# Moving three waits in a fused two-block transformer kernel: one forget product per level, diagonal copies ahead, first heads on the first query fill

## The chip, the cores and the metric

The kernel runs on one core of one Trainium2 chip. The metric is the device time of one execution in microseconds; 972.3 us is the median of three runs before the change (971.54, 972.3, 977.76).

## What is computed

Two transformer blocks over 256 tokens of width 1024, in float32. The first (convolution and retention, then a feed-forward and a gated projection) is not touched. The second normalises x and multiplies it by one wide input matrix; the columns of the product feed three branches, which are merged, projected and followed by a convolutional feed-forward. The branch of the change is HGRN2, a gated linear attention that runs forwards and backwards over the tokens, 8 heads of 128:

```python
h = rmsnorm_2(x, norm_mix[l])
(hq, hi, hff, hfb, hg, nq, nk, nv, cq, g_hg, g_na, g_ca) = split_cols(h @ w_in[l])
y_hg = hgrn2_branch(hq, hi, hff, hfb, hg, lower_bounds[l], hg_gnorm[l], w_hg_o[l])
y_na = neighbourhood_attention(nq, nk, nv, na_rpb[l], w_na_o[l])
y_ca = memory_cross_attention(cq, mem_n, w_mem_kv[l], w_ca_o[l])
...
# in hgrn2_branch, for either direction
f = lb_d + (1.0 - lb_d) * jax.nn.sigmoid(zf)
log_f = jnp.log(jnp.maximum(f, F_FLOOR))
k = (1.0 - lb_d) * jax.nn.sigmoid(-zf)
...
# in gla_chunk_scan: token t sees token s through the product of the forgets between them
scores = jnp.einsum('bhtk,bhsk,bhtsk->bhts', qc, kc, decay)
```

The cross attention is ordinary: 4 heads of 128, queries cq, keys and values from a memory of 256 tokens. The neighbourhood attention has 8 heads of 64.

## The kernel before

**Weights.** They stream from memory in units of 8 blocks of 128 x 128 (raw). ScalarE casts a unit to its high part w_hi (L627), DVE (L1022) or POOL (L590) subtracts to get the low part w_lo, and TensorE multiplies high and low parts in three passes. Four units are held (w_hi, w_lo), so the cast of a unit waits until TensorE has used the one four before it. A "fill" is the product of h with the weights of one piece of the columns (16 blocks, 48 matmuls) into one of three PSUM banks (ring), and an engine reads the bank out. On ScalarE, `wait_fill` casts the units up to a target (`split_target`), waits for the fill, and casts those that its end has set free (`behind_target`).

**The order of the second block.** The fills come in the order hq, hff, hfb (queries and forgets), then the sixteen "side fills" hi 0 to 3, hg 0 to 3, nq, nk, nv, cq (two each), then the merge fills mhg, mca, mna (eight each). Every engine runs through the same list of side fills and does its part of the HGRN2 scores between them, by `DIAGONAL_AFTER = 1`, `LEVEL_AFTER = {1: 0, 3: 1, 5: 2, 7: 3, 9: 4, 11: 5, 12: 6}` and `CROSS_AFTER = 13`. So after fill hi 1 come the diagonal and level 0, after hi 3 level 1, after hg 1 level 2, and so on.

**The levels.** The scores of two tokens are built by halving: at level i (half width b = 1, 2, ..., 64) the token pairs that lie in the two halves of a span of 2b are filled in. The steps of a level:
- ScalarE, `level_keys`: waits until the forgets and keys of the level are there (`level_ready`), then makes the mixed keys in two copies (L683, into gate_tmp and k_mix). It sits in `wait_fill`, ahead of the wait for the fill.
- TensorE, `level`: 64 small matmuls in four groups (L1831) into four banks (sc); group g waits for its key copy and, at level 0, for ScalarE's copy of the diagonal of that group (`st_diag`), later for DVE's masks of the level before.
- DVE, `masks`: copies the banks under a mask into st_hg (L1344), eight in all. `grow`: four products of 1024 elements carry queries and keys to the next level (L1360 to L1363), a wait for the last of them, and then the forget product of the forward direction (L1364) and of the backward direction (L1365), every 2b-th element by its partner b further on; the second one signals `level_ready`.

The diagonal (`diagonal` on TensorE, L1811, 16 products) stands right behind fill hi 1 and ahead of level 0; on ScalarE its four copies (L864) stand behind the weight cast and the value copy of hi 1 (L700).

**After the levels.** `cross` and `hg_values` give the outputs o_hg, which DVE gates and normalises (L1379, L1385, L1389) and splits (L1036) for the fill mhg 0. Fills cq 0 and cq 1 follow on TensorE; ScalarE copies each into its half of q_ca (L700). The attention heads go in slots between the merge fills, four cross heads first (`att_slot`): scores of a head (L1898), DVE's maximum (L1414, L1416), ScalarE's exponential (L915), DVE's normalisation (L1421, L1423), TensorE's transposes (L1908) and, a slot later, its products with the values (L1933, L1923). Head i reads head i's part of q_ca; fill cq 0 holds heads 0 and 1. Slot 0 stands between fill cq 1 and fill mhg 0.

SyncE loads a table for the neighbourhood attention once the last forget product has been signalled; POOL masks it between low parts.

Of the kernel before, what the change touches and what calls it, by code (L numbers as in the profile page):

```python
# [198 lines left out]
def program(nc, x_tok, mem_tok, pt, wstream, wproj, vecs, gains, consts, rope_tab, decay_tab, rpb, out, toep):  # L199
    ctx = ExitStack()  # L200
    with ctx:
# [43 lines left out]
        def at(kib, name, *shape, dt=F32):  # L245
            assert 1024 * kib + 4 * np.prod(shape) <= 1024 * ARENA_KIB, name
            return place(name, list(shape), dt, offset=arena + int(1024 * kib))
# [27 lines left out]

        f_f = at(0, "f_f", HG, S)
        f_b = at(8, "f_b", HG, S)
        k_fb = at(16, "k_fb", 2, HG, S)
# [177 lines left out]
        def wait_read(eng, name, j):  # L456

            n = fi(name, j)
            eng.wait_ge(freed[FILLS[n][3]], freed_count(n, FILLS[n][3]))
# [154 lines left out]
        def _(act):  # L614
# [61 lines left out]
            def level_keys(i):  # L676


                b = LEVELS[i]
                act.wait_ge(level_ready, i + 1)  # L680
                for half in range(2):
                    dst = k_mix[half].rearrange("p a s -> p (a s)").rearrange("p (n two b) -> p n two b", two=2, b=b)
                    nc.scalar.copy(dst, partners(k_f[:, 4 * half:4 * half + 4], b)).then_inc(mix_keys, 1)  # L683

            def wait_fill(name, j, behind=True):

                n = fi(name, j)
                feed(split_target(n))
                side = n - fi("hi", 0)
                if side in LEVEL_AFTER:  # L690
                    level_keys(LEVEL_AFTER[side])
                act.wait_ge(pe_step, fill_step(n))
                if behind:
                    feed(behind_target(n))
# [194 lines left out]

            for e, (name, j) in enumerate(SIDE_FILLS):  # L890
                if name in ("hi", "nv"):
                    dst = (v_hg if name == "hi" else v_na)[:, :, 256 * j:256 * j + 256]
                    copy_fill(name, j, dst)
                elif name == "hg":
                    copy_fill(name, j, gate_hg[:, 2 * j:2 * j + 2], ACT.Silu)
                else:
                    copy_fill(name, j, {"nq": q_na, "nk": k_na, "cq": q_ca}[name][:, 2 * j:2 * j + 2])
                if e == DIAGONAL_AFTER:
                    diagonal()
                if e == CROSS_AFTER:  # L900
                    cross()
                    hg_outputs()
                if e >= CROSS_AFTER:
                    hg_hi_part(e - CROSS_AFTER)
# [88 lines left out]
        def _(dve):  # L993
# [353 lines left out]
            def grow(i):  # L1347
# [7 lines left out]
                nb = HG * S // (2 * b)  # L1355
                fa, fb_ = halves(f_f[:])
                ba, bb_ = halves(f_b[:])
                bc = lambda t: t[:, :, 0:1].to_broadcast([P, nb, b])
# [4 lines left out]
                after(link(V.tensor_tensor(kb, kb, bc(ba), ALU.mult)))  # L1363
                V.tensor_tensor(fa[:, :, 0:1], fa[:, :, 0:1], fb_[:, :, 0:1], ALU.mult)  # L1364
                V.tensor_tensor(ba[:, :, 0:1], ba[:, :, 0:1], bb_[:, :, 0:1], ALU.mult).then_inc(level_ready, 1)  # L1365
                dve.wait_ge(level_ready, i + 2)
# [172 lines left out]
        def _(pe):  # L1539
# [339 lines left out]
            def att_scores(a):  # L1879
# [12 lines left out]
                if a < 2:  # L1892
                    pe.wait_ge(hg_root, 4)
                    wait_read(pe, "cq", 1)
                else:
                    pe.wait_ge(exp_ready, a - 1)
                for t in range(2):
                    last = mm(sc[a % 2][:, t * S:t * S + S], q_ca[:, i, t * P:t * P + P], mem_k[:, i, :],  # L1898
                              start=True, stop=True)
# [195 lines left out]
```

## Time and profile before

| | |
|---|---|
| median of three runs | 972.3 us |
| profiled execution | 973.71 us, of which 971.9 us span |
| TensorE busy | 936.8 us, 96% |
| DVE, ScalarE, POOL busy | 688.4, 518.2, 371.1 us |
| mean granted TensorE clock | 0.995 |

How to read it: the levels stand between 478 and 585 us, the merge fills with the heads between 607 and 703. The page's shares are averages over the whole program, and TensorE is the busiest engine in nearly every slice; what an edit is worth is read from the pieces of the chain of waits in its own stretch, and from the brackets in an engine's timeline, which say how long it was idle before an instruction and what released it. A piece called "issue" waited for nothing that the profile names. Matmuls are pipelined, so a matmul's row may start before the one ahead of it has ended.

### The profile page before, as it was taken

To read this page: it belongs to the slowest core of one execution; us is meant where nothing else is said; L and a number is where in the kernel's file an instruction comes from. 1 tells how busy PE (TensorE), PEld (TensorE's weight loads), DVE (VectorE), ACT (ScalarE), POOL (GpSimd) and SP (SyncE) were. 2 spreads that over 40 slices of the span, in tenths; PEclk is the share of its full clock that TensorE was granted. 3 is DMA by queue.
4 is the path that set the end of the run, shared out by engine and by line. 5 is a ranking of instruction groups with operands and counts; after the bars stand their busy time and mean duration, and the time that the engine had idled before them with its cause. 6 is when DMAs were issued, how large, how long until landed. Compare 5 with 4: busy or idle time off the path is not lost.

```text
span 971.9 us, 15074 instructions
## 1 busy us (share of the span) xinstructions
PE 936.8 (96%) x6118; PEld 848.7 (87%) x6118; DVE 688.4 (71%) x886; ACT 518.2 (53%) x790; POOL 371.1 (38%) x136
## 2 busy tenths in 40 slices
PE   7999999999999999999999999999899999999997
PEld 6998986888888878999999998999799878888885
DVE  4998586688884257567598977875545569999722
ACT  6853465545444356555444445554544556666632
POOL 0000000556664400002555533555686236566541
PEclk9999999999999999999999999999999999999999
DMA  9652344555556544545523325443355455555551
GB/s 354 216 204 87 141 136 161 202 176 195 193 174 216 176 171 174 174 171 177 174 87 131 130 93 157 152 142 130 102 194 204 137 176 186 182 207 175 185 205 44
DMA packets 30437, 162.57 MB, mean 167 GB/s; under 512 B 9089, under 2 KB 9489, under 8 KB 11936
## 3 DMA queue, kind: packets, MB, share of 16 engines
q1 hardware_dynamic: 30304, 161.53, 48.4%
q8 instruction: 49, 0.80, 0.3%
q14 instruction: 20, 0.16, 0.1%
q0 software_dynamic: 64, 0.08, 0.0%
HBM read 160.48 MB, written 1.12 MB: 166 GB/s over the span
## 4 chain that ended last, share of the span: by engine, by line
PE 86%; DVE 8%; ACT 4%; issue 2%; DMA 1%; SPq 0%; DVEq 0%; ACTq 0%
PE ring L1579 28%; PE acc L1657 18%; PE acc L1591 9%; PE ring L1591 8%; PE ring L1610 5%; PE acc L1592 4%; PE ring L1592 4%; PE acc L1831 3%; PE acc L1692 1%; ACT w_hi L627 1%; DVE w_lo L1022 1%; DVE y L1074 1%; DMA gain_mix_pre<-gains 1%; PE ring L1692 1%; DVE ret_inv L1185 1%
## 5 line engine op out<-in xcount | busy, mean ns | idle before, releaser
L590 POOL TENSOR_TENSOR w_lo<-raw,w_hi 128x1024 fp32r<-128x1024 f32 x124 | 359.2, 2902 | 580.3 <-ACT w_hi L627 580.2
L627 ACT CAST w_hi<-raw 128x1024 fp32r<-128x1024 f32 x284 | 296.7, 1050 | 322.3 <-PE ring L1579 120.4
L1022 DVE TENSOR_TENSOR w_lo<-raw,w_hi 128x1024 fp32r<-128x1024 f32 x160 | 202.6, 1275 | 107.2 <-ACT w_hi L627 97.0
L1579 PE MATMUL ring<-h,w_hi 128*128 128x256 f32 x1408 | 257.4, 285 | 3.7 <-DVE w_lo L1022 1.8
L1579 PEld LDWEIGHTS ring<-h,w_hi 128*128 128x128 f32 x1408 | 219.7, 192 | 6.7 <-issue 3.1
L1579 PE MATMUL ring<-h,w_lo 128*128 128x256 f32 x704 | 199.1, 283 | 0.0
L1579 PEld LDWEIGHTS ring<-h,w_lo 128*128 128x128 f32 x704 | 135.0, 192 | 0.0
L1591 PE MATMUL acc<-h,w_hi 128*128 128x512 f32 x352 | 125.9, 400 | 2.9 <-DVE h L1080 2.9
L1591 PE MATMUL ring<-h,w_hi 128*128 128x512 f32 x352 | 124.2, 396 | 0.0
L1592 PE MATMUL acc<-h,w_lo 128*128 128x256 f32 x352 | 99.0, 281 | 0.0
L1592 PE MATMUL ring<-h,w_lo 128*128 128x256 f32 x352 | 98.2, 279 | 0.0
L1657 PE MATMUL acc<-w_hi,ff 128*128 128x512 f32 x352 | 94.3, 390 | 0.0
L1591 PEld LDWEIGHTS acc<-h,w_hi 128*128 128x128 f32 x352 | 66.9, 190 | 19.4 <-DVE h L1080 2.0
L1591 PEld LDWEIGHTS ring<-h,w_hi 128*128 128x128 f32 x352 | 66.1, 188 | 15.9
L1657 PEld LDWEIGHTS acc<-w_hi,ff 128*128 128x128 f32 x352 | 65.8, 188 | 13.8 <-DVE w_lo L1022 0.2
L1241 DVE TENSOR_TENSOR ff<-prod_tmp,ff 128x256 fp32r<-128x256 f32 x44 | 67.2, 1529 | 0.9 <-ACT ff L985 0.9
L1592 PEld LDWEIGHTS acc<-h,w_lo 128*128 128x128 f32 x352 | 67.0, 190 | 0.0
L1592 PEld LDWEIGHTS ring<-h,w_lo 128*128 128x128 f32 x352 | 66.3, 188 | 0.0
L1657 PE MATMUL acc<-w_lo,ff 128*128 128x512 f32 x176 | 54.2, 389 | 0.0
L1610 PE MATMUL ring<-w_hi,h 128*128 128x256 f32 x256 | 46.9, 285 | 0.8 <-ACT v_ret L700 0.8
L1248 DVE TENSOR_REDUCE ring<-acc 128x512 f32<-128x1024 f32 x22 | 27.1, 1233 | 22.2 <-PE acc L1592 22.2
L1610 PEld LDWEIGHTS ring<-w_hi,h 128*128 128x128 f32 x256 | 40.0, 192 | 1.1 <-ACT v_ret L700 1.0
(251 smaller groups left out, 1395.0 us busy)
## 6 DMA issues: line engine op xcount, KB each, us to landing
raw<-wstream SPq DMA_DIRECT2D x142, 1024.0 KB, 4.8
toep_t<-toep SPq DMA_DIRECT2D x16, 96.0 KB, 3.2
x<-x_tok SPq DMA_DIRECT2D x2, 512.0 KB, 5.2
mem<-mem_tok SPq DMA_DIRECT2D x1, 1024.0 KB, 12.4
w_ple<-wproj SPq DMA_DIRECT2D x1, 1024.0 KB, 7.4
out_t<-y SPq DMA_DIRECT2D x4, 256.0 KB, 2.4
decay<-decay_tab SPq DMA_DIRECT2D x1, 768.0 KB, 7.2
gain_mix_pre<-gains SPq DMA_DIRECT2D x1, 512.0 KB, 7.2
```

Of the source, the lines that this page charges most:

```text
L590: nc.gpsimd.tensor_tensor(w_lo[:, u % UNITS], unit_of_raw(u), as_f32(w_hi[:, u % UNITS]), ALU.subtract).then_inc(lo_ready["pool"], 1)
L627: nc.scalar.copy(w_hi[:, u % UNITS], unit_of_raw(u)).then_inc(hi_ready, 1)
L1022: V.tensor_tensor(w_lo[:, u % UNITS], unit_of_raw(u), as_f32(w_hi[:, u % UNITS]), ALU.subtract).then_inc(lo_ready["dve"], 1)
L1241: V.tensor_tensor(ff[:, 1, j], prod_tmp[:, j % 2], as_f32(ff[:, 0, j]), ALU.subtract).then_inc(ff_ready, 1)
L1248: V.tensor_reduce(bank(name, j), b.rearrange("p i a s -> p i s a"), AX.X, ALU.add).then_inc(summed, 1)
L1579: last = mm(dst, w[a], src[:, b, kt], start=n == 0 and i == 0, stop=n == kts - 1 and i == 2)
L1591: mm(both, w[0], h_both[:, kt].rearrange("p a s -> p (a s)"), start=kt == 0, stop=False)
L1592: last = mm(b[:, i, 0], w[1], h[:, 0, kt], start=False, stop=kt == KT - 1)
L1610: last = mm(b[:, tt], src[:, xa, kt, tt * P:tt * P + P], ws[kt][wa], start=kt == 0 and i == 0, stop=kt == KT - 1 and i == 2)
L1657: last = mm(acc[:, tt, 512 * g:512 * g + 512], src(b, i, tt), w[:, u % UNITS, 4 * g:4 * g + 4].rearrange("p a b -> p (a b)"), start=i == 0 ...
L1692: last = mm(out, diag[:, w], conv_in[:, t, w:w + S], start=w == first, stop=w == end - 1)
L1831: last = mm(sc[g][:, c:c + P], tile(k_mix[g // 2], 2 * (g % 2) + a, tt), q, start=True, stop=True)
```

## The change

Three edits:

1. f_f and f_b become the two halves of one tensor f_fb at the same addresses. The two forget products of a level become one of twice the elements, and that one signals `level_ready`.
2. ScalarE waits for fill hi 1 and makes the four diagonal copies first; the cast that the end of the fill sets free and the value copy follow. `level_keys` counts its calls, so that the second `wait_fill` for the same fill does not repeat the keys.
3. TensorE's scores of heads 0 and 1 wait for ScalarE's read of fill cq 0 instead of cq 1; the wait for cq 1 moves to head 2.

```diff
-        f_f = at(0, "f_f", HG, S)
-        f_b = at(8, "f_b", HG, S)
+        f_fb = at(0, "f_fb", 2, HG, S)
+        f_f, f_b = f_fb[:, 0], f_fb[:, 1]
...
             def level_keys(i):
 
+                level_keys.done += 1
...
+            level_keys.done = 0
+
             def wait_fill(name, j, behind=True):
...
-                if side in LEVEL_AFTER:
+                if side in LEVEL_AFTER and LEVEL_AFTER[side] == level_keys.done:
                     level_keys(LEVEL_AFTER[side])
...
             for e, (name, j) in enumerate(SIDE_FILLS):
+                if e == DIAGONAL_AFTER:
+                    wait_fill(name, j, behind=False)
+                    diagonal()
                 if name in ("hi", "nv"):
...
-                if e == DIAGONAL_AFTER:
-                    diagonal()
                 if e == CROSS_AFTER:
...
-                fa, fb_ = halves(f_f[:])
-                ba, bb_ = halves(f_b[:])
+                fa, fb_ = halves(f_f)
+                ba, bb_ = halves(f_b)
...
-                V.tensor_tensor(fa[:, :, 0:1], fa[:, :, 0:1], fb_[:, :, 0:1], ALU.mult)
-                V.tensor_tensor(ba[:, :, 0:1], ba[:, :, 0:1], bb_[:, :, 0:1], ALU.mult).then_inc(level_ready, 1)
+                both = f_fb[:].rearrange("p d a s -> p (d a s)").rearrange("p (n two b) -> p n two b", two=2, b=b)
+                first, second = both[:, :, 0, 0:1], both[:, :, 1, 0:1]
+                V.tensor_tensor(first, first, second, ALU.mult).then_inc(level_ready, 1)
...
                 if a < 2:
                     pe.wait_ge(hg_root, 4)
-                    wait_read(pe, "cq", 1)
+                    wait_read(pe, "cq", 0)
                 else:
                     pe.wait_ge(exp_ready, a - 1)
+                if a == 2:
+                    wait_read(pe, "cq", 1)
```

ScalarE around the diagonal, behind the fill hi 1, before the change:

```order
L627 CAST w_hi<-raw 128x1024 [waits pe_step,slot_ready0]
L683 COPY gate_tmp<-k_fb 128x1024 [waits level_ready]
L683 COPY k_mix<-k_fb 128x1024
L627 CAST w_hi<-raw 128x1024 [waits pe_step]
L700 COPY v_hg<-ring 128x2x256
L864 COPY st_hg<-acc 128x2x2x128 [waits sc_done] x4
L627 CAST w_hi<-raw 128x1024 [waits pe_step,slot_ready1]
```

and with the change (lines have moved by some):

```order
L627 CAST w_hi<-raw 128x1024 [waits pe_step,slot_ready0]
L685 COPY gate_tmp<-k_fb 128x1024 [waits level_ready]
L685 COPY k_mix<-k_fb 128x1024
L868 COPY st_hg<-acc 128x2x2x128 [waits sc_done,pe_step]
L868 COPY st_hg<-acc 128x2x2x128 [waits sc_done] x3
L627 CAST w_hi<-raw 128x1024 [waits pe_step]
L704 COPY v_hg<-ring 128x2x256
```

The four copies into st_hg have passed one cast and one value copy; the first cast and the key copies stay where they were.

DVE at the end of level 1, before (q_bf and k_fb are the queries and keys of both directions, f_f and f_b the forgets):

```order
L1360 TENSOR_TENSOR q_bf<-q_bf,f_f 128x512x2
L1361 TENSOR_TENSOR k_fb<-k_fb,f_f 128x512x2
L1362 TENSOR_TENSOR q_bf<-q_bf,f_b 128x512x2
L1363 TENSOR_TENSOR k_fb<-k_fb,f_b 128x512x2
L1364 TENSOR_TENSOR f_f<-f_f 128x512 [waits dve_chain]
L1365 TENSOR_TENSOR f_b<-f_b 128x512
L1022 TENSOR_TENSOR w_lo<-raw,w_hi 128x1024 [waits hi_ready,level_ready]
```

and with the change:

```order
L1365 TENSOR_TENSOR q_bf<-q_bf,f_fb 128x512x2
L1366 TENSOR_TENSOR k_fb<-k_fb,f_fb 128x512x2
L1367 TENSOR_TENSOR q_bf<-q_bf,f_fb 128x512x2
L1368 TENSOR_TENSOR k_fb<-k_fb,f_fb 128x512x2
L1371 TENSOR_TENSOR f_fb<-f_fb 128x1024 [waits dve_chain]
L1027 TENSOR_TENSOR w_lo<-raw,w_hi 128x1024 [waits hi_ready,level_ready]
```

Two products of 512 elements have become one of 1024, and nothing else has moved; the other levels differ in the same way.

## Rows read from the trace of the kernel before

**Rows 1.** The page, part 1: busy us (share of the span) and instructions.
```profile
PE 936.8 (96%) x6118; PEld 848.7 (87%) x6118; DVE 688.4 (71%) x886; ACT 518.2 (53%) x790; POOL 371.1 (38%) x136
```
**Rows 2.** Chain of waits, 455 to 640 us: start us, us, what.
```profile
479.16 5.53 PE acc L1831 x32
484.69 11.50 PE ring L1610 x96
496.19 0.86 issue
...
529.42 0.57 issue
...
570.02 1.14 issue
```
**Rows 3.** TensorE's timeline: start us, us, instruction, [idle before <-releaser].
```profile
475.75 2.40 PE L1811 MATMUL acc<-y,sq 128*128 128x128 f32 x20
...
514.10 2.02 PE L1831 MATMUL acc<-q_bf,gate_tmp 128*128 128x128 f32 x16 [1.46 <-issue]
```
**Rows 4.** ScalarE's timeline, 470 to 590 us.
```profile
477.01 1.04 ACT L627 CAST w_hi<-raw 128x1024 fp32r<-128x1024 f32 x1
...
478.44 2.02 ACT L864 COPY st_hg<-acc 128x512 f32<-128x512 f32 x4
...
495.81 1.15 ACT L683 COPY gate_tmp<-k_fb 128x1024 f32<-128x1024 f32 x1
...
509.86 1.05 ACT L627 CAST w_hi<-raw 128x1024 fp32r<-128x1024 f32 x1
...
526.63 1.05 ACT L627 CAST w_hi<-raw 128x1024 fp32r<-128x1024 f32 x1 [1.33 <-PE ring L1579]
```
**Rows 5.** DVE's timeline at the ends of levels 1, 4 and 5.
```profile
505.25 1.22 DVE L1363 TENSOR_TENSOR k_fb<-k_fb,f_b 128x1024 f32<-128x1024 f32 x1
506.50 3.20 DVE L1364 TENSOR_TENSOR f_f<-f_f 128x512 f32<-128x512 f32 x1
...
554.51 2.37 DVE L1364 TENSOR_TENSOR f_f<-f_f 128x64 f32<-128x64 f32 x1
...
569.64 0.23 DVE L1364 TENSOR_TENSOR f_f<-f_f 128x32 f32<-128x32 f32 x1
```
**Rows 6.** POOL's timeline in levels 0 and 1.
```profile
478.13 2.36 POOL L590 TENSOR_TENSOR w_lo<-raw,w_hi 128x1024 fp32r<-128x1024 f32 x1 [3.06 <-ACT w_hi L627]
...
505.23 6.73 POOL L590 TENSOR_TENSOR w_lo<-raw,w_hi 128x1024 fp32r<-128x1024 f32 x2 [3.73 <-ACT w_hi L627]
```
**Rows 7.** Chain of waits at the first heads.
```profile
608.34 0.49 ACT q_ca L700
...
616.69 0.44 PE acc L1908 x4
...
623.75 0.44 PE acc L1908 x4
```
**Rows 8.** DVE's timeline at the first heads.
```profile
611.26 1.45 DVE L1036 TENSOR_TENSOR o_hg_s<-o_hg,o_hg_s 128x512 fp32r<-128x512 f32 x2
...
614.81 0.62 DVE L1423 TENSOR_SCALAR probs<-probs,soft 128x256 f32<-128x256 f32 x2
...
620.76 1.76 DVE L1423 TENSOR_SCALAR probs<-probs,soft 128x256 f32<-128x256 f32 x2
```
**Rows 9.** TensorE's timeline among the heads.
```profile
608.97 1.10 PE L1898 MATMUL acc<-mem_k,q_ca 128*128 128x256 f32 x4 [1.77 <-ACT q_ca L700]
...
675.33 1.08 PE L1923 MATMUL acc<-probs_t,v_na 128*64 128x256 f32 x8
...
689.47 1.12 PE L1908 MATMUL acc<-con,probs 128*128 128x128 f32 x4 [2.59 <-DVE probs L1423]
690.52 1.98 PE L1923 MATMUL acc<-probs_t,v_na 128*64 128x256 f32 x8
```
**Rows 10.** Busy us of PE, PEld, DVE, ACT, POOL; granted clock; DMA share, GB/s.
```profile
690.00:693.00 3.00, 3.00 (x15) 1.54 (x14) 2.67 (x4) 0.26 (x1) 2.35 (x1) 0.60 0.00 0
```

## The prediction

> **What bounds the kernel now.** I read the page's first part, then the chain of waits in the two stretches that the change touches, and last the engines' own timelines there. TensorE is busy 96% of the span [rows 1]. So an edit is worth only what it takes out of TensorE's gaps; a cheaper DVE or ACT operation in a covered stretch is worth nothing. The reader should see in the chain [rows 2] how few gaps there are: TensorE's level products (L1831) alternate with fills (L1610, L1579). Ahead of level 0 it waits 1.01 us, from 478.15, where the diagonal products end (475.75 + 2.40 in [rows 3]), to 479.16. Ahead of level 1 the "issue" piece is 0.86 us, of level 3 0.57, of level 6 1.14 [rows 2]. Ahead of level 2 the chain runs over DVE, so the gap is the bracket of [rows 3], 1.46 us. Levels 4 and 5 have none to speak of. Together that is 5.0 us. The second touched place is the first cross head, ahead of which TensorE is idle for 1.77 us [rows 9]. The whole reach of the change is thus 6.8 us, 0.7% of the time.
>
> **Diagonal copies ahead of weight and value.** Nothing is added on ScalarE or taken from it; the four L864 copies (2.02 us together) move ahead of a weight cast (1.04 us) and a value copy. Before, the key copies end as the cast starts, at 477.0, and the first diagonal copy starts at 478.44 [rows 4]; level 0 starts when it has landed, at 479.16. Afterwards the first diagonal copy starts near 477.1 and ends near 477.7. TensorE is busy with the diagonal products until 478.15, and ScalarE's pitch of 0.5 us is shorter than a group of level 0 (5.53 / 4 = 1.4 us), so the later groups do not wait either: **1.0 us** gained. The cast starts near 479.1 in place of 477.01. Queued behind it is POOL's low part of the same unit (2.36 us from 478.13 [rows 6]), which then ends near 482.6. Its reader is the fill hi 3, half way through the 11.50 us piece that begins at 484.69 [rows 2], near 490.4: 7.8 us of cover. The value copy frees a bank that is wanted only three fills after its own. Both moves cost nothing; with that cover gone, the price would be the 2.1 us of the move.
>
> **One forget product per level.** DVE loses seven instructions of 886. What counts is when the last product ends, since ScalarE's key copies wait for it, and TensorE for the first key copy.
> - *What the product costs.* At levels 1 and 4 the forward product takes 3.20 and 2.37 us, for 512 and 64 elements; at level 5 it takes 0.23 us for 32, and L1363 takes 1.22 us for 1024 [rows 5]. So the operation itself is short, and at levels 1 to 4 some 2.4 us of each product is something else. POOL's low part takes 2.36 us, and two of them (6.73 us from 505.23) cover the stretch in which the two products of level 1 stand [rows 6]. I read it so: POOL gets in when DVE drains for the chain wait after L1363, DVE's first product goes next, then POOL's second low part, and DVE's second product waits again. With one product there is one wait. At level 1 that makes 3.20 + 0.55 (512 more elements, by the 1.22 us for 1024) = 3.75 us, where the pair took 3.20 and as much again, 6.4; at level 2, between the rows of levels 1 and 4, about 3.1 instead of 5.5.
> - The Trainium skill bears on this twice. "SBUF — State Buffer", section "Who interferes with whom", says that a VectorE instruction with two SBUF inputs and a GpSimd instruction that reads SBUF exclude each other for the whole instruction. The same page, in the section on Door 1, says that accesses which cross to a new 16-byte line pay a penalty, and from level 1 on every element of these products lies on a line of its own. By the first rule the merger saves a wait of some 2.4 us per level; by the second it saves next to nothing, for the merged product would last as long as both.
> - I take the reading with POOL, because the step from 2.37 us for 64 elements to 0.23 us for 32 is too steep for a cost per element.
> - *Level 1* (gap 0.86) gains nothing: its key copy starts at 495.81 with no idle bracket, straight behind a cast, so ScalarE was not waiting for DVE [rows 4].
> - *Level 2* (gap 1.46): the merged product ends at 506.50 + 3.75 = 510.25 instead of 512.9. Late next is ScalarE's cast, 509.86 + 1.05 = 510.91; a key copy of 1.15 us ends at 512.1, ahead of the 514.10 - 1.46 = 512.64 at which TensorE is free. The whole **1.46 us** goes.
> - *Level 3* (gap 0.57): before, TensorE starts at 529.99, one key copy and 0.1 us after the product. The product ends 2.4 us earlier, near 526.4; the cast of 526.63 ends at 527.7 [rows 4] and the key copy at 528.8, ahead of 529.42. **0.57 us** goes.
> - *Level 6* keeps nearly all of its 1.14 us, since the products before it (from 569.64) are the short ones: one fewer saves **0.1 us**.
>
> Bounds for this part: 0.3 us (0.1 at each of the three gaps that DVE ends) if the product keeps both durations, 2.1 us as worked out. I take 2.1, by the short row of level 5.
>
> **First heads wait for the first query fill.** ScalarE copies cq 1 from 608.34 to 608.83 [rows 7], behind a weight cast; the scores of head 0 read cq 0's half only. TensorE can start them at the end of the fill, about **1.7 us** earlier, and the fill mhg 0 with them. Late next is the softmax of head 0. DVE is busy with the gated outputs until 611.26 + 1.45 = 612.71 and ends L1423 of head 0 at 614.81 + 0.62 = 615.43 [rows 8]; nothing in that chain starts earlier. TensorE's transposes (L1908) stood at 616.69 [rows 7], 1.26 us later; now they would be reached near 614.96, so a wait of 0.5 us replaces part of the old one. The added wait, at the third head, is for a copy done at 608.83 and read after 622: nothing. One slot on, DVE ends at 620.76 + 1.76 = 622.52 against transposes at 623.75: 1.23 us of cover, and since that slot's work follows the end of TensorE's fill, about half of the shift reaches DVE too. So 1.7 - 0.5 = **1.2 us**. Bounds: 0 (DVE stays late in all slots) and 1.7; I take 1.2, the value that the rows of the first slot give.
>
> **Sum.** 1.0 + 1.46 + 0.57 + 0.1 + 1.2 = 4.3 us. The profiled execution took 973.71 us, 971.9 of them span; the same execution would take 969.4. It lies 1.4 us above the median of the runs, 972.3; from there 4.3 us less is 968.0. About 1% (9.7 us) is what a measurement of this kernel can tell from no change, so the forecast is inside that.
>
> **The rivals.**
> 1. *The product's time is its own.* If the 2.4 us is the elements' stride and not POOL, the gaps of levels 2 and 3 stay, less 0.1 each. For it: every slow product is strided. Against it: the 32-element product, strided wider still. Gain 1.0 + 0.3 + 1.2 = 2.5 us: 969.8.
> 2. *The attention gives it back.* DVE's softmax, about 1.2 us ahead of TensorE in the first slots, becomes the limit in one of them; a low part on POOL that falls on L1423 suffices. Once this already costs a gap of 2.59 us [rows 9]. For it: L1423 takes 1.76 us in one slot and 0.62 in another [rows 8]. Against it: DVE's work follows the ends of TensorE's fills, so both shift. One such gap eats 2.6 of the 4.3 us: 970.6.
> 3. *Slower.* The same place, with the clock. Behind the gap of 2.59 us the granted clock was 0.60 from 690 to 693 [rows 10] (of 2.4 GHz, so a part of it at the 1.2 GHz level), and the value products took 1.98 us instead of 1.08, the transposes 1.12 [rows 9], some 0.5 more than elsewhere: 1.4 us. A slot that turns out so costs 4.0 us. One new slot of that kind cancels the gain (968.0 + 4.0 = 972.0), and from the second on the kernel is slower: 968.0 + 8.0 = 976.0. For it: after the change TensorE comes to each slot earlier against a DVE that is not faster. Against it: among the twelve heads only this one slot turned out so before.
> 4. *More than the forecast.* POOL's and DVE's low parts meet differently, and the gap at 689.47 vanishes with its clock loss: 968.0 - 4.0 = 964.0.
>
> That the change does not do what it says I can leave out: the order of the instructions shows each part.
>
> **How the numbers follow.** The forecast (965.5 to 969.5) has 0.56, rival 1 0.12, rival 2 0.17, rival 3 0.08, rival 4 0.07. Rivals 1 and 2 and a part of rival 4 belong in the range, and the runs of before differ by themselves (971.54 to 977.76): 964.8 to 972.8. Over 1% faster needs 9.7 us, so the whole reach of 6.8 us and rival 4 on top: 0.03. Over 1% slower needs four slots of rival 3 or a disturbed measurement: 0.03. Within 1%: 0.94.
>
> **What would show it.** Right: level 0 starts straight behind the diagonal products; the gaps ahead of levels 2 and 3 vanish, those of levels 1 and 6 stay; one product of about 3.7 us at level 1 and 2.5 us at level 4; DVE's busy time falls by some 12 us (a wait of 2.4 us less at each of levels 0 to 4), of which only 2.1 us reach the end; the scores of head 0 follow their fill at once, and a gap of 0.5 us stands ahead of its transposes. Wrong: merged products as long as both old ones, or a gap of over 2 us among the heads that was not there.

## The result and the profile after

The median of ten runs is 970.11 us (966.44 to 971.49); the kernel before, run beside it on the same chip, has 973.75 us (971.54 to 977.76). The ratio is 0.9949 with a 95% interval of 0.9929 to 0.9968: 3.1 to 6.9 us faster, within 1%. The forecast was 968.0 us, in a range of 964.8 to 972.8. The profiled execution took 967.13 us, 965.3 of them span.

The page of the changed kernel, part 1, answers to [rows 1], and the first line of part 4 says which engines the chain of waits ran over.

```profile
PE 935.4 (97%) x6118; PEld 848.9 (88%) x6118; DVE 679.9 (70%) x879; ACT 517.6 (54%) x790; POOL 372.9 (39%) x136
...
PE 88%; DVE 6%; ACT 3%; issue 1%; DMA 1%; SPq 0%; DVEq 0%; ACTq 0%
```

TensorE's work is the same and its gaps are fewer. The chain of waits of the changed kernel, 440 to 640 us (start us, us, what), answers to [rows 2] and, in its last three lines, to [rows 7]. TensorE's level products are L1837 now, the diagonal is L1817, the scores L1906, the transposes L1916.

```profile
472.87 3.57 PE acc L1817 x32
476.44 5.30 PE acc L1837 x32
481.74 11.50 PE ring L1616 x96
493.24 0.86 issue
494.10 4.08 PE acc L1837 x32
498.18 11.52 PE ring L1585 x96
509.69 3.57 PE acc L1837 x32
513.27 11.52 PE ring L1585 x96
524.78 3.57 PE acc L1837 x32
...
564.28 1.07 issue
565.35 3.81 PE acc L1837 x32
...
601.40 0.87 PE acc L1906 x4
602.27 5.77 PE ring L1585 x48
609.71 0.66 PE acc L1916 x4
```

The gaps ahead of levels 0, 2 and 3 are gone (472.87 + 3.57 = 476.44, 498.18 + 11.52 = 509.70, and so on); those of levels 1 and 6 stand at 0.86 and 1.07 us. The scores of head 0 follow their fill at once. What is new is between 602.27 + 5.77 = 608.04 and 609.71: a piece of TensorE's work and a wait, which its timeline gives as 0.82 us.

```profile
609.71 0.66 PE L1916 MATMUL acc<-con,probs 128*128 128x128 f32 x4 [0.82 <-DVE probs L1429]
```

DVE's timeline of the changed kernel, at the ends of levels 0, 1, 2, 4 and 5 and at head 0, answers to [rows 5, 8].

```profile
487.10 2.29 DVE L1371 TENSOR_TENSOR f_fb<-f_fb 128x2048 f32<-128x2048 f32 x1
...
503.55 4.16 DVE L1371 TENSOR_TENSOR f_fb<-f_fb 128x1024 f32<-128x1024 f32 x1
508.06 3.00 DVE L1027 TENSOR_TENSOR w_lo<-raw,w_hi 128x1024 fp32r<-128x1024 f32 x1 [0.36 <-ACT w_hi L627]
...
518.63 3.22 DVE L1371 TENSOR_TENSOR f_fb<-f_fb 128x512 f32<-128x512 f32 x1
...
548.80 2.48 DVE L1371 TENSOR_TENSOR f_fb<-f_fb 128x128 f32<-128x128 f32 x1
...
563.89 0.28 DVE L1371 TENSOR_TENSOR f_fb<-f_fb 128x64 f32<-128x64 f32 x1
...
603.71 1.86 DVE L1395 TENSOR_TENSOR o_hg<-o_hg,hg_sq 128x512 f32<-128x512 f32 x1
...
609.04 0.61 DVE L1429 TENSOR_SCALAR probs<-probs,soft 128x256 f32<-128x256 f32 x2
```

At level 1 one product of 4.16 us stands where two of 3.20 and 3.32 stood (6.42 us from the start of the first to the end of the second). The low part behind it takes 3.00 us now, where the one behind the pair took 1.22. ScalarE's timeline shows the reordered diagonal and, at level 2, who is late now.

```profile
475.31 2.02 ACT L868 COPY st_hg<-acc 128x512 f32<-128x512 f32 x4
...
477.22 1.06 ACT L627 CAST w_hi<-raw 128x1024 fp32r<-128x1024 f32 x1
...
506.91 1.05 ACT L627 CAST w_hi<-raw 128x1024 fp32r<-128x1024 f32 x1
507.87 1.04 ACT L685 COPY gate_tmp<-k_fb 128x1024 f32<-128x1024 f32 x1
```

The diagonal copies stand ahead of the cast. The key copy of level 2 starts behind the cast of 506.91, not behind the product, and ends at 508.91, 0.8 us before TensorE wants it at 509.69.

**A ruler for small differences.** The fill hi 0 starts at 462.88 us of the span in the kernel before and at 461.19 after, though nothing ahead of it was changed; over the 14 traces of this study it starts between 461.2 and 467.0. So I measure every kernel from that start. In a stretch that an edit leaves alone, the distances then agree to 0.05 us. The starts are those of TensorE's timeline; a row with no gap ahead of it starts 0.16 us or more before the one ahead has ended.

| us from the start of fill hi 0 to | before | after | gained in all |
|---|---|---|---|
| level 0 | 16.28 | 15.09 | 1.19 |
| level 1 | 34.17 | 32.91 | 1.26 |
| level 2 | 51.22 | 48.34 | 2.88 |
| level 3 | 67.11 | 63.43 | 3.68 |
| level 6 | 108.28 | 104.16 | 4.12 |
| scores of head 0 | 146.09 | 140.05 | 6.04 |
| transposes of head 0 | 153.65 | 148.52 | 5.13 |
| first output product of the feed-forward (L1663 now) | 287.42 | 282.56 | 4.86 |

The change gains 4.9 us in its stretch, and 1.7 of the 6.6 us between the two spans lie ahead of it, in code that is the same.

### The profile page after: what moved, and what is told of

The parts are those of the page before. It is cut to its first block, busy times and chain, and to the rows that moved or that the text cites. A ratio compares the mean times of both kernels' runs of the same rounds, so it can differ in the third digit from the quotient of the medians.

```text
span 965.3 us, 15069 instructions
## 1 busy us (share of the span) xinstructions
PE 935.4 (97%) x6118; PEld 848.9 (88%) x6118; DVE 679.9 (70%) x879; ACT 517.6 (54%) x790; POOL 372.9 (39%) x136
## 4 chain that ended last, share of the span: by engine, by line
PE 88%; DVE 6%; ACT 3%; issue 1%; DMA 1%; SPq 0%; DVEq 0%; ACTq 0%
PE ring L1585 30%; PE acc L1663 18%; PE acc L1597 9%; PE ring L1597 8%; PE ring L1616 5%; PE acc L1598 4%; PE ring L1598 4%; PE acc L1837 3%; PE acc L1698 1%; DVE w_lo L1027 1%; ACT w_hi L627 1%; DVE y L1079 1%; PE ring L1698 1%; DVE ret_inv L1190 1%; ACT sq L633 1%
## 5 line engine op out<-in xcount | busy, mean ns | idle before, releaser
L1027 DVE TENSOR_TENSOR w_lo<-raw,w_hi 128x1024 fp32r<-128x1024 f32 x160 | 205.8, 1295 | 116.3 <-ACT w_hi L627 106.0
L1663 PE MATMUL acc<-w_hi,ff 128*128 128x512 f32 x352 | 94.3, 390 | 0.0
L1663 PEld LDWEIGHTS acc<-w_hi,ff 128*128 128x128 f32 x352 | 65.8, 188 | 13.8 <-DVE w_lo L1027 0.2
L1663 PE MATMUL acc<-w_lo,ff 128*128 128x512 f32 x176 | 54.2, 389 | 0.0
```

Source lines behind the costliest of these rows:

```text
L1027: V.tensor_tensor(w_lo[:, u % UNITS], unit_of_raw(u), as_f32(w_hi[:, u % UNITS]), ALU.subtract).then_inc(lo_ready["dve"], 1)
L1663: last = mm(acc[:, tt, 512 * g:512 * g + 512], src(b, i, tt), w[:, u % UNITS, 4 * g:4 * g + 4].rearrange("p a b -> p (a b)"), start=i == 0 ...
```

## The experiments

**Each part alone.** The first three runs take one of the three edits each, on the kernel before.

```diff
-                V.tensor_tensor(fa[:, :, 0:1], fa[:, :, 0:1], fb_[:, :, 0:1], ALU.mult)
-                V.tensor_tensor(ba[:, :, 0:1], ba[:, :, 0:1], bb_[:, :, 0:1], ALU.mult).then_inc(level_ready, 1)
...
+                V.tensor_tensor(first, first, second, ALU.mult).then_inc(level_ready, 1)
```

> The kernel before with the first edit alone (one forget product per level). My theory: the gaps ahead of levels 2 and 3 vanish (1.46 and 0.57 us before) and with each the slower start behind it (0.24 us), level 0 keeps its 1.0, level 1 its 0.86, level 6 about 1.07 us; from the end of level 0 to the end of the fill cq 1 the kernel before takes 122.5 us, so here 119.7; the first cross head keeps its 1.77. The whole kernel 2.5 to 3 us shorter. Rival (DVE's time does not matter, the gaps close only together with the other edits): the gaps stay.

Measured: 971.23 us against 974.34, ratio 0.9959 (0.9942 to 0.9976). By the ruler, 2.87 us by the transposes of head 0. The gaps ahead of levels 2 and 3 go, and the one ahead of head 0's scores stays at 1.77.

```diff
...
+                if e == DIAGONAL_AFTER:
+                    wait_fill(name, j, behind=False)
+                    diagonal()
...
-                if e == DIAGONAL_AFTER:
-                    diagonal()
```

> The kernel before with the second edit alone (diagonal copies ahead of weight and value). My theory: level 0 starts straight behind the diagonal products, 1.0 us of gap and 0.2 of slow start gone, all other gaps as before (1.46, 0.57, 1.14, 1.77); the whole kernel 1.2 us shorter. Rival (the delayed cast is paid for later): a new gap of up to 2 us ahead of the fills hi 2 or hi 3.

Measured: 973.06 us, ratio 0.9995 (0.9971 to 1.0018): the total sees nothing. The ruler does: 1.25 us.

```diff
-                    wait_read(pe, "cq", 1)
+                    wait_read(pe, "cq", 0)
...
+                if a == 2:
+                    wait_read(pe, "cq", 1)
```

> The kernel before with the third edit alone (first heads wait for cq 0). My theory: the gap of 1.77 us ahead of head 0's scores goes, one of 0.8 us ahead of the transposes of head 0 comes, net 1.0 us shorter up to the second slot, later slots as before. Rival (the softmax loses more when the levels before it are late): a gap of over 1.5 us at the transposes and nothing gained.

Measured: 972.74 us, ratio 0.9983 (0.9964 to 1.0002); 1.04 us by the ruler, with a gap of 0.84 us ahead of the transposes. The three parts add up to 2.87 + 1.25 + 1.04 = 5.16 us; all together gave 5.13. They neither help nor hinder each other.

**What the product's time is made of.** I had read the slow products as a wait for POOL. This run, on the changed kernel, gives POOL's low parts between hg 2 and nq 1 to DVE. POOL is then idle at levels 1 and 2. My expectation counts level 3 among the idle ones, but the edit does not reach its low parts; POOL works there and at level 4 as before, and both serve as the control.

```diff
+    if _within(u, [(INDEX[("hg", 2)], INDEX[("nq", 1)])]):
+        return "dve"
```

> The changed kernel with the low parts of the fills hg 2 to nq 1 on DVE instead of POOL, so that POOL is idle around the forget products of levels 1 to 3, and busy as before at level 4. Theory (the product waits for a low part of POOL that runs): the product of level 1 takes about 1.2 us instead of 4.16, that of level 2 about 0.65 instead of 3.22, level 3 about 0.4 instead of 2.70, level 4 still 2.4 to 2.5. Rival (a fixed cost of such a strided product, whatever POOL does): 4.1, 3.2, 2.7 as in the changed kernel. The kernel as a whole may be slower, since DVE has more to do and does it ahead of the masks.

DVE's timeline of this kernel, at the ends of levels 1 to 4:

```profile
506.53 2.08 DVE L1373 TENSOR_TENSOR f_fb<-f_fb 128x1024 f32<-128x1024 f32 x1
...
522.30 1.20 DVE L1373 TENSOR_TENSOR f_fb<-f_fb 128x512 f32<-128x512 f32 x1
...
539.60 2.71 DVE L1373 TENSOR_TENSOR f_fb<-f_fb 128x256 f32<-128x256 f32 x1
...
552.66 2.48 DVE L1373 TENSOR_TENSOR f_fb<-f_fb 128x128 f32<-128x128 f32 x1
```

and POOL's, idle from 501.50 on:

```profile
499.12 2.38 POOL L592 TENSOR_TENSOR w_lo<-raw,w_hi 128x1024 fp32r<-128x1024 f32 x1 [2.12 <-ACT w_hi L629]
535.44 6.41 POOL L592 TENSOR_TENSOR w_lo<-raw,w_hi 128x1024 fp32r<-128x1024 f32 x2 [33.93 <-ACT w_hi L629]
```

With POOL idle the products take 2.08 and 1.20 us where the changed kernel has 4.16 and 3.22: 2.1 and 2.0 us less. The controls stay (2.71 and 2.48 at levels 3 and 4, where the changed kernel has 2.70 and 2.48). So each product does wait for one low part of POOL. But its own time is no trifle either: 2 ns per element here, against 2.29 us for 2048 elements, 1.1 ns, at level 0, where the step from one pair to the next is two elements and no wait is seen. I had expected 1.2 and 0.65 us. The rival with the stride was right in that the stride costs time, and wrong about the wait. The time was 969.31 us in one run. By the ruler the kernel takes 0.9 us more to head 0's transposes: with more to do, DVE comes 0.7 us later to level 3, POOL's low part now meets the last key product there too (3.43 us instead of 1.22), and a gap of 0.64 us stands ahead of level 4. This is no improvement.

**Does POOL get in because DVE drains?** Here the forgets move to packed halves of a second buffer, so that the product follows the key product without a chain wait, and its operands lie closer from level 1 on.

```diff
+        f_ping = at(72, "f_ping", HG * S)
...
-                after(link(V.tensor_tensor(kb, kb, bc(ba), ALU.mult)))
...
-                V.tensor_tensor(first, first, second, ALU.mult).then_inc(level_ready, 1)
+                V.tensor_tensor(kb, kb, bc(ba), ALU.mult)
+                V.tensor_tensor(nxt.unsqueeze(2), now[:, :, 0:1], now[:, :, 1:2], ALU.mult).then_inc(level_ready, 1)
```

> The changed kernel, but each level's forget product is written to another buffer, closely packed, so that DVE needs no chain wait between the last key product and the forget product. Same sums, same output. Theory (POOL gets in only where DVE drains for that wait): the product of levels 1 to 4 takes 1.2, 0.7, 0.4 and 0.3 us although POOL has a low part waiting, and POOL's part runs after it; the gaps of TensorE stay as in the changed kernel, since DVE is no longer the last. Rival (POOL's part takes its turn between any two DVE instructions): the product or one of the four before it still takes 2.4 us more.

DVE's timeline of this kernel at the end of level 1, and POOL's there:

```profile
504.13 1.22 DVE L1374 TENSOR_TENSOR k_fb<-k_fb,f_ping 128x1024 f32<-128x1024 f32 x1
505.27 3.43 DVE L1375 TENSOR_TENSOR f_fb<-f_ping 128x1024 f32<-128x1024 f32 x1
```

```profile
504.12 6.84 POOL L591 TENSOR_TENSOR w_lo<-raw,w_hi 128x1024 fp32r<-128x1024 f32 x2 [3.78 <-ACT w_hi L628]
```

The product starts with no break behind L1374 and still takes 3.43 us, the product of level 2 2.89. POOL's low part asks at 504.12, as L1374 starts; L1374 runs at its usual 1.22 us, and the instruction behind it waits for all of POOL's. The drain is not what lets POOL in: that part of my reading falls, and the rival holds. The closer packing takes 4.16 - 3.43 = 0.7 us off level 1's product.

I could have read this in the kernel before. No wait stands between L1364 and L1365, and yet at level 0 POOL's low part, which asks while L1364 runs, gets in between them. DVE's and POOL's timelines there:

```profile
490.06 1.23 DVE L1364 TENSOR_TENSOR f_f<-f_f 128x1024 f32<-128x1024 f32 x1
491.20 3.44 DVE L1365 TENSOR_TENSOR f_b<-f_b 128x1024 f32<-128x1024 f32 x1
```

```profile
490.21 6.68 POOL L590 TENSOR_TENSOR w_lo<-raw,w_hi 128x1024 fp32r<-128x1024 f32 x2 [9.72 <-ACT w_hi L627]
```

Two products of the same size take 1.23 and 3.44 us. The time of the kernel without the drain was 968.42 us in one run, beside 976.0 for the kernel before.

**The gap ahead of level 1.** ScalarE's key copies of level 1 are called ahead of the weight cast instead of behind it.

```diff
+                side = n - fi("hi", 0)
+                now = side in LEVEL_AFTER and LEVEL_AFTER[side] == level_keys.done
+                if now and side == 3:
+                    level_keys(LEVEL_AFTER[side])
                 feed(split_target(n))
-                side = n - fi("hi", 0)
-                if side in LEVEL_AFTER and LEVEL_AFTER[side] == level_keys.done:
+                if now and side != 3:
                     level_keys(LEVEL_AFTER[side])
```

> The changed kernel with the key copies of level 1 ahead of the weight cast that waits for TensorE. Theory (at level 1 the key copy stands behind that cast, not behind DVE): the merged product of level 0 ends 2.5 us before the cast could start, the copies run there, the gap of 0.86 us goes with 0.2 of slow start, 1.1 us shorter. Rival (TensorE waits for something else there): 0.86 stays.

ScalarE's timeline of this kernel ahead of level 1:

```profile
491.53 1.18 ACT L685 COPY gate_tmp<-k_fb 128x1024 f32<-128x1024 f32 x1 [0.33 <-DVE f_fb L1374]
492.60 1.17 ACT L685 COPY k_mix<-k_fb 128x1024 f32<-128x1024 f32 x1
493.99 1.05 ACT L627 CAST w_hi<-raw 128x1024 fp32r<-128x1024 f32 x1 [0.21 <-PE ring L1619]
```

The key copy waits for the product (0.33 us) and no more for the cast, and the gap is gone: level 1 starts 31.90 us behind hi 0 instead of 32.91, and 1.1 us are still there at level 6 and at head 0. The total of the one run, 970.45 us, shows nothing of it.

**The gap ahead of level 6.** DVE makes the two key products first and signals them, so that ScalarE's copies need not wait for the query products and the forget product.

```diff
-                act.wait_ge(level_ready, i + 1)
+                if i:
+                    act.wait_ge(keys_scaled, i)
...
-                V.tensor_tensor(qf, qf, bc(fa), ALU.mult)
                 V.tensor_tensor(kf, kf, bc(fb_), ALU.mult)
-                V.tensor_tensor(qb, qb, bc(bb_), ALU.mult)
-                after(link(V.tensor_tensor(kb, kb, bc(ba), ALU.mult)))
+                V.tensor_tensor(kb, kb, bc(ba), ALU.mult).then_inc(keys_scaled, 1)
+                V.tensor_tensor(qf, qf, bc(fa), ALU.mult)
+                after(link(V.tensor_tensor(qb, qb, bc(bb_), ALU.mult)))
```

> The changed kernel with the two key products of a level ahead of the two query products, and a signal of their own to ScalarE's key copies. Theory (the gap ahead of level 6, 1.07 us, is one key copy behind the end of the forget product): that copy now runs beside the query products, the gap falls to 0.1 us or nothing, and the slow start behind it goes: 1.1 to 1.3 us shorter. Level 1 keeps its 0.86. Rival (ScalarE's cast of the same stretch is the last): the gap stays near 1 us.

ScalarE's timeline of this kernel ahead of level 6, and TensorE's:

```profile
565.58 1.05 ACT L628 CAST w_hi<-raw 128x1024 fp32r<-128x1024 f32 x1 [6.36 <-PE ring L1620]
566.53 1.04 ACT L689 COPY gate_tmp<-k_fb 128x1024 f32<-128x1024 f32 x1
```

```profile
567.67 1.58 PE L1841 MATMUL acc<-q_bf,gate_tmp 128*128 128x128 f32 x12 [0.75 <-issue]
```

The gap falls from 1.07 to 0.75 us only, since the copy now stands behind a cast that waited for TensorE. Two things were late, one behind the other, and of the 1.1 to 1.3 us expected the ruler shows 0.3. The time of the one run was 968.85 us.

**The gap ahead of head 0's transposes.** The last reciprocal of the gated outputs is cut from 512 elements to 32; this kernel leaves out the rest of that norm.

```diff
-                            V.reciprocal(root_g, root_g).then_inc(hg_inv, 1)
+                            part = root_g if g < 4 else root_g[:, :, 0:16]
+                            V.reciprocal(part, part).then_inc(hg_inv, 1)
```

> The changed kernel with the reciprocal of the last pair of heads in the gated outputs cut to 16 of 256 columns (the rest of that norm is left out), so that DVE comes to the softmax of head 0 about 3 us earlier. Theory (the gap of 0.82 us ahead of head 0's transposes is DVE being late by its gated outputs): that gap goes and the kernel is 0.8 to 1.0 us shorter up to the second slot. Rival (ScalarE's table load or the slot's own chain sets it): the gap stays.

DVE's timeline of this kernel behind the short reciprocal, and POOL's:

```profile
603.76 0.34 DVE L1392 RECIPROCAL hg_sq<-hg_sq 128x32 f32<-128x32 f32 x1
604.13 2.49 DVE L1396 TENSOR_TENSOR o_hg<-o_hg,hg_sq 128x512 f32<-128x512 f32 x1
...
607.01 3.03 DVE L1041 TENSOR_TENSOR o_hg_s<-o_hg,o_hg_s 128x512 fp32r<-128x512 f32 x2 [0.38 <-ACT o_hg_s L892]
```

```profile
603.16 5.72 POOL L590 TENSOR_TENSOR w_lo<-raw,w_hi 128x1024 fp32r<-128x1024 f32 x2 [0.48 <-ACT w_hi L627]
```

Three microseconds less work on DVE took only 0.34 off the gap (0.83 to 0.49). In the changed kernel the long reciprocal, with its single input, covered most of POOL's two low parts (599.74 to 605.02); without that cover they fall on the two-input instructions behind it, 2.49 and 3.03 us instead of 1.86 and 1.46. These two and the wait of 0.38 us between them take back 2.6 of the 3.0 us.

**Both key edits, and the changed kernel again.** The next kernel has the edits of the two level runs together; beside it the changed kernel ran once more.

> The changed kernel with both further edits (level 1's key copies ahead of the cast; key products first at every level). Theory: no gap above 0.1 us is left ahead of any level, 2.2 to 2.4 us less than the changed kernel; ratio to the kernel before about 0.9925 against 0.995 of the changed kernel. Rival (the attention takes it back): the levels gain and the slots lose it.

> The changed kernel again, beside the one with both further edits on the same chip: 0.993 to 0.997 of the kernel before; its trace again has gaps of 0.86 (level 1), 1.07 (level 6) and 0.82 (head 0's transposes) and none at levels 0, 2 and 3. What differs from its first trace outside the second block's levels and heads is then what varies by itself from run to run.

Measured: 969.21 and 969.88 us beside 973.87, ratios 0.9945 (0.9926 to 0.9965) and 0.9954 (0.9938 to 0.997). By the ruler the first is 1.42 us shorter by head 0's transposes (147.12 against 148.54), yet the totals cannot be told apart. That is short of the 2.2 to 2.4 us expected, since the gap of 0.75 us ahead of level 6 stays, as in the run before. The changed kernel repeats itself: 0.86, 1.07, 0.83 and 2.60 us of gaps where its first trace has 0.86, 1.07, 0.82 and 2.61, and a further gap of 0.70 in a late slot.

That further gap is no loss. TensorE's products with the values behind the gap of 2.6 us, first in the first trace of the changed kernel and then in the second:

```profile
683.68 1.98 PE L1931 MATMUL acc<-probs_t,v_na 128*64 128x256 f32 x8
```

```profile
684.45 1.08 PE L1931 MATMUL acc<-probs_t,v_na 128*64 128x256 f32 x8
```

In the first the granted clock is 0.54 over three microseconds there (0.50, the 1.2 GHz level, over the first two of them), in the second it stays at 1.00. TensorE then comes 1.4 us earlier to the next slot and waits 0.70 us for the softmax, and 0.6 us are gained in the end. TensorE was idle for 2.6 us just before in either trace. Of the 14 traces 12 have a clock of 0.50 to 0.65 there, and the two with 1.00 (this one and the one with the key products first) are the two with the further gap.

**No gap at the levels.** The key copies go ahead of the cast at level 6 too.

```diff
-                if now and side == 3:
+                if now and side in (3, 12):
                     level_keys(LEVEL_AFTER[side])
                 feed(split_target(n))
-                if now and side != 3:
+                if now and side not in (3, 12):
```

> The kernel with both further edits, and ScalarE's key copies ahead of its weight cast at level 6 too. Theory (there the cast that waits for TensorE is the last since the key products come first): no gap of TensorE is left ahead of any level, level 6's 0.75 us and its slow start of 0.2 us go; from the start of fill hi 0 to the transposes of head 0 146.1 to 146.2 us, where the changed kernel takes 148.5 and the one with both edits 147.1. Rival: the later cast makes a gap of up to 1 us ahead of a following fill. Ratio to the kernel before 0.992 to 0.996.

Measured: 968.1 us beside 974.15, ratio 0.994 (0.9915 to 0.9964). No level waits any more, but TensorE's timeline shows a new gap, small, ahead of the cross products:

```profile
575.72 0.49 PE L1854 MATMUL acc<-q_bf,k_fb 128*128 128x128 f32 x2 [0.35 <-DVE f_fb L1378]
```

By the ruler 146.55 us to head 0's transposes, 2.0 less than the changed kernel, where 146.1 to 146.2 was expected. What waits next are the cross products, for DVE's last forget product (L1378).

**A low part behind the softmax.** On top of that, the last weight unit of mhg 1 gets its low part from DVE, and behind the softmax of head 0 instead of on POOL ahead of it.

```diff
 def _lo_engine(u):
+    if u == FIRST_BLOCK[INDEX[("mhg", 1)] + 1] // UB - 1:
+        return "dve"
...
-                feed_behind(name, j)
+                if e < 15:
+                    feed_behind(name, j)
+                else:
+                    feed(behind_target(fi(name, j)) - 1)
```

> The same, and the low part of the last unit of fill mhg 1 on DVE, behind the softmax of head 0, instead of on POOL, where it made DVE's gated outputs wait. Theory (of the gap of 0.83 us at head 0's transposes all is that wait, 1.17 us at L1395 of the changed kernel): the gap goes, 0.8 us less up to the second slot. Rival (DVE's additional 1.2 us comes back in the next slot): a gap of 0.1 to 1 us at head 1's transposes. Ratio to the kernel before 0.991 to 0.995.

Measured: 965.58 us beside 974.15, ratio 0.9916 (0.9887 to 0.9946), the lowest median here. DVE's and TensorE's timelines of it:

```profile
604.38 0.69 DVE L1407 TENSOR_TENSOR o_hg<-o_hg,hg_sq 128x512 f32<-128x512 f32 x1
...
609.07 2.35 DVE L1036 TENSOR_TENSOR w_lo<-raw,w_hi 128x1024 fp32r<-128x1024 f32 x2
```

```profile
609.38 0.60 PE L1928 MATMUL acc<-con,probs 128*128 128x128 f32 x4
...
616.82 0.66 PE L1928 MATMUL acc<-con,probs 128*128 128x128 f32 x4 [0.22 <-DVE probs L1441]
```

The product of the gated outputs falls from 1.86 to 0.69 us, head 0's transposes wait for nothing, and head 1's by 0.22 us. By the ruler 145.56 us to head 0, 1.0 less than the kernel above and 3.0 less than the changed kernel; of that 1.0 the transposes of head 1 keep 0.7 and those of the later heads 0.6, so part of it comes back, as the rival said. The interval to the kernel before lies wholly below 0.995. Against the changed kernel itself there is no direct interval; the traces say 3.0 us at head 0 and 2.6 at the later heads, the medians 4.3 to 4.5, but they are from different chips.

## Why the prediction held, step by step

**What bounds the kernel.** Right, and the parts alone show it: TensorE's gaps set what each edit was worth. DVE lost 8.5 us of busy time, of which the levels gave 2.9 to the end.

**Diagonal copies, forecast 1.0 us.** Measured 1.25 alone and in the whole. The gap went as worked out, and the later cast cost nothing. The further 0.24 us is explained below.

**The forget product, forecast 1.46 + 0.57 + 0.1 = 2.1 us.** Measured 2.87. The gaps of levels 2 and 3 went and those of levels 1 and 6 stayed (1.14 became 1.07), as forecast. Two inputs to this step were off and did no harm. The product at level 1 took 4.16 us, not 3.75: I took one rate for all spacings (L1363's 1.2 ns per element, of which 512 elements make 0.61 us and not my 0.55), where the strided product alone needs 2 ns. And the reason "POOL gets in when DVE drains" is wrong; the run without the drain has the same wait. What stands is one wait of about 2 us per product, and one product fewer is one wait fewer. The Trainium skill, "SBUF — State Buffer", section "Who interferes with whom", has both engines exclude each other for the whole instruction; the trace agrees, with 2.08 us against 4.16 for the same product. The forecast of 12 us for DVE holds for the products alone: their rows sum to 27.6 us before and 15.4 after. DVE's busy time fell by only 8.5 us, because POOL's second low part now falls on DVE's own low part behind the product (3.00 us behind level 1's product where it was 1.22, 2.06 behind level 2's where it was 1.23): the rows of the low parts grew from 202.6 to 205.8 us. That DVE would pay part of the wait elsewhere was missing in the forecast; here it was paid where nothing waited for it.

**First heads, forecast 1.7 - 0.5 = 1.2 us.** Measured 1.98 gained at the scores and 1.04 given back at the transposes, 0.94 net (1.04 in the run of this edit alone). Nothing more was given back in the slots behind, and the wait for cq 1 at head 2 shows no gap. The mechanism was right and the new gap mis-sized, 0.82 us for 0.5. Most of that 0.3 is that TensorE came to the transposes 2.0 us earlier and not 1.7 (the term of the next paragraph); DVE came 0.06 us later.

**The term that was missing.** The same work of TensorE takes longer behind a gap, at the same granted clock of 1.00:

| piece | behind a gap | without |
|---|---|---|
| level 0 | 5.53 (before) | 5.30 (after) |
| level 1 | 4.08 (after) | 3.85 (key copies ahead) |
| level 2 | 3.81 (before) | 3.57 (after) |
| scores of head 0 | 1.10 (before) | 0.87 (after) |
| transposes of head 0 | 0.66 (after) | 0.44 (before) |

The step is 0.22 to 0.24 us each time, whatever the gap's length (0.57 to 1.77 us). Level 4 had it too (3.81 before, 3.57 after) behind a gap of 0.03 us. With it the sum comes out: levels 0, 2, 3 and 4 give 4 x 0.24 = 0.96 us on top of the 3.1 forecast, where 4.1 was measured. At head 0 TensorE gains 1.77 + 0.23 = 2.00 and gives back 0.82 + 0.22 = 1.04. Level 6 looks like an exception: 3.81 behind its gap and 3.80 in the kernel that has none. But there its first product starts 0.22 us behind the start of the last one of the fill, where 0.12 is the pace at level 2 (509.41 to 509.53), and its first sixteen products take 2.05 us instead of 1.95: TensorE still waited for some 0.2 us that no bracket shows.

The rows say where most of the step comes from. A gap is counted from the end of the last matmul, but without a wait the next one would have started before that end: at level 2 of the changed kernel the fill's last matmul ends at 509.69 and the level's first starts at 509.53. That is 0.16 us of the 0.24; the other 0.07 to 0.08 us lie in the level's first sixteen products (2.02 us instead of 1.95), and no run isolates their cause.

**The rivals.** The product's time as its own (1) fell with the run that left POOL idle, half of its reason surviving: at a step of four elements the own time is nearly twice what I took. The attention giving it back (2) and a further slot at a low clock (3) did not come. The gap of 2.59 us stayed, at 2.61 in the changed kernel, with a granted clock of 0.54 behind it, and so rival 4 fell as well. Its clock loss, though, is no fixed price of that gap: in the second trace of the same kernel the clock stayed at 1.00, as told above, and of the 1.4 us of rival 3 only 0.6 was gained, as DVE was late next.

**The total.** Forecast -4.3 us; the medians say -3.6 and the ratio -5.0 (3.1 to 6.9); the ruler, which leaves out what was not touched, says -4.9. That is about 0.6 us more than my sum: 1.0 more at the levels and 0.3 less at the heads, with the rest lost on the way to L1663. That the sum came so near is in part luck, since the missing term and the mis-sized gap have opposite signs. The time itself was forecast at 968.0 us and came out at 970.11: 1.45 of the 2.1 us are the base, 972.3 by three runs and 973.75 by ten.

## What to carry to other kernels

When TensorE is busy 96% of the span, list its gaps and name for each the one that is late next; three edits judged so gave what their gaps held, to a few tenths. A removed gap is worth its length plus, here, 0.23 us, and a new gap costs the same on top. For edits of a microsecond in a program of a thousand, read the distance between two fixed points of the trace around the edit; the total told apart neither the diagonal nor the heads edit alone, nor the two key edits. A stretch at a low clock can come and go in the same kernel, so take two traces before you count one as gained or lost. Before shortening an instruction on DVE, look at what POOL does beside it: an operation with one input may be the cover under which POOL's work costs nothing, while one of these low parts, moved behind the critical softmax, gained 1.0 us there and 0.6 further on.

## What the runs showed of the hardware

- *Two-input DVE instructions and POOL.* A POOL subtraction of 128x1024 that asks while DVE issues two-input instructions back to back gets its turn behind the one that is about to run (asked 504.12, L1374 from 504.13 for 1.22 us, then 2.3 us of waiting in L1375), or behind the one that runs (asked 490.21, L1364 from 490.06 for 1.23 us, then 2.2 us of waiting in L1365). I had expected it to need a pause in DVE's stream.
- *Spacing.* In-place products of single elements took 1.1 ns per element at a step of two elements from pair to pair (2.29 us for 2048), and 2.0 to 2.3 ns at steps of four and eight (2.08 us for 1024, 1.20 for 512); none of the three waited for POOL. The short ones point to a fixed part of about 0.2 us: 0.28 us for 64 elements, 0.23 for 32, and 0.20 for 16 in the kernel before.
- *The start behind a gap*, 0.23 us, as above.
- *The clock behind a gap.* After the same 2.6 us of idle time the granted clock fell to 0.50 to 0.65 over three microseconds in 12 traces and stayed at 1.00 in two, one of them of the changed kernel, whose other trace has 0.54.
- *Where repeated runs differ.* In fills that are the same code, one piece of 384 matmuls in the chain of waits takes 46.51 us from 16.52 in the kernel before and 47.99 us from 15.77 in the changed one. The second has a granted clock of 0.97 over the first 60 us, the first 1.00, and pays 1.5 us. Of the windows 0 to 60 us, first of the kernel before and then of the changed one (busy us of PE, granted clock, DMA share, GB/s):

```profile
0.00:60.00 60.00, 53.46 (x425) 1.00 0.74 272
```

```profile
0.00:60.00 60.00, 54.51 (x419) 0.97 0.73 268
```

  In the diagonal run the clock was 0.86 between 168 and 180 us, and its execution took 979.04 us against a median of 973.06. With the clock at 0.89 from 165 to 180 us, the second trace of the changed kernel reached fill hi 0 at 462.33 against 461.19. In both the clock is lowest just behind two idle times of TensorE, 0.70 and 1.11 us (0.55 from 171 to 174 us in the diagonal run, 0.54 from 168 to 171 us in the second trace), which the traces without a fall have as well. These stretches lie before anything that the change touches; what lets the clock fall in one run and not in the next stays open.
